# Attention by pairs of maps on row tiles of TensorE, values as weights, and the convolution's taps moved into the input projection

## The chip, the cores and the metric

The kernel runs on one core of a Trainium2 chip, in one launch. The time is the device time of that launch in microseconds; smaller is better. The core has TensorE (PE in the profile), VectorE (DVE), ScalarE (ACT), GpSimd (POOL) and SyncE (SP). Each engine runs its own list of instructions in order, and they meet at semaphores. Transfers run on 16 DMA engines, which the queues of SP, ACT and POOL feed.

## The reference

Two layers of a transformer step for 512 latent tokens and 128 context tokens of width 1024, all in f32. A layer is, in short:

```python
h = _rms(x, p['norm1_g']) * (1.0 + sc1) + sh1
u = h @ p['w_in']
qa, ka, va, pool_in, glu_in, qd, kd, vd = jnp.split(u, SPLIT_POINTS, axis=-1)
# A: 4 query heads on 2 key heads of 64, q/k norm, rotary:  p = softmax(s); o = p @ v
# D: 4 heads, two maps each (32 features):  p = softmax(s1) - lam * softmax(s2); o = p @ v, then _rms over 64
# B: means over windows of 2, 4, 8, 16 tokens, minus x, times pool_w
# C: a * sigmoid(gate), 31-tap depthwise convolution, norm over 256 channels, silu, pw_w
m = jnp.concatenate([o_a, o_b, o_c, o_d], axis=-1) @ p['w_out']
x = x + g1 * m
h2 = _rms(x, p['norm2_g']) * (1.0 + sc2) + sh2
x = x + g2 * _expert_choice_ffn(h2, ...)   # 16 experts, top-k tokens each, SwiGLU
```

Shift, scale and gate (sh, sc, g) are six products of silu(c) with w_mod. Latent queries see 128 cached keys and 512 latent keys, context queries the 128 context keys. So there are 12 score maps (4 of A, 8 of D) for each of 4 latent row tiles of 128 x 640, and 12 of 128 x 128 for the context tile.

## The kernel before

Tokens stand in five row tiles of 128 (`t` = 0 to 3 latent, 4 context). A layer runs in five phases, with a barrier over all four computing engines at the end of each (`finish_phase`).

Phase 1, the input projection. The order of its steps is written by hand (`ORDER` for TensorE, `TAKE_ORDER` for the engines that empty PSUM). "x": a tile of x, already scaled by VectorE, is turned by 8 transposes (L399) and taken into `H` (features x tokens), half by ScalarE (L805), half by VectorE (L1082). "s": squares of a later x tile (L797). "j": 24 matmuls of a row tile with w_in give q, k, v (L422 to L424), then squares, root on GpSimd (L1389), gains and rotary. "q": seven transposes bring q and k into `qkT`. "f": the pooling and convolution columns come out with features on the partitions (L453, L454), last of all. x has two buffers.

Phase 2, attention. For each map TensorE multiplies a query tile, spread by GpSimd so that rows of other heads are zero (L1448, L1452), with all 128 rows of keys (L486 latent keys, L487 cached keys). VectorE takes the maximum (L1178), ScalarE the exponential with its sum (L877), TensorE turns the map in five chunks (L500), ScalarE copies them out (L885), and TensorE multiplies with the values, the turned map as weights and 64 value columns moving (L517). Once a row tile VectorE divides by the sums, subtracts the second maps and, with GpSimd's root, norms the differential heads; four transposes (L525) put the outputs into `H`. Between maps VectorE does the convolution's taps (L1214, 47 of 62), GpSimd the pooling sums and the other 15 taps (L1496, L1497).

Phase 3: mean and variance of the convolution by matmuls with `mean_w` (L560), norm, the modulations GATE1 and SCALE2 (L361), Silu, point-wise and pooling matmuls, and, among them, 16 instructions of the first tile's output projection (L547).

Phases 4 and 5: output projection, second norm, router, top-k; then a loop over 16 experts (L659, L667), whose weights stream through the six slots of `ring`.

## Time and profile before

| | us |
|---|---|
| median of 3 runs (lowest, highest) | 2118.03 (2117.74, 2120.58) |
| the profiled execution | 2116.8 |
| its span | 2114.7 |
| TensorE busy, of the span | 1922.1 |
| VectorE / ScalarE / GpSimd busy | 558.8 / 514.5 / 456.3 |
| mean granted TensorE clock | 0.948 |

The page gives TensorE as busy for 91% of the span, but that is a mean over stages of different kinds: the expert loops (530 to 1060 us and from 1558 us on) hold half of the span, with DMA at 99% or more in most slices. The stages of the change are from 36 to 400 us and from 1068 to 1435 us. A busy TensorE in them says that it sets the pace only where its instructions follow each other without a gap and the others wait for it, so the timeline and the idle times of the other engines are read beside the busy share.

### The profile page before, as it was taken

Reading aid. Unit: us, or ns where it says so; the run is one execution under the profiler, and the core shown is the slowest. Engines: PE = TensorE matmul, PEld = TensorE weight load, DVE = VectorE, ACT = ScalarE, POOL = GpSimd, SP = SyncE. Lnnn points to the kernel's source line nnn. Section 1 sums busy time; section 2 is a strip of 40 time slices with the busy share of each in tenths; the row PEclk is TensorE's granted clock in tenths of the full one; section 3 lists DMA queues with packets and bytes.
Section 4 is the critical chain, followed back from the end, with each engine's and each line's share of the span. In section 5 each row is a group of like instructions: output and inputs, shape, how many; then the busy total and the mean of one; then the engine's idle time right before and its main releaser. Section 6 shows DMA issues by size and latency. Waiting matters only on the chain.

```text
span 2114.7 us, 40059 instructions
## 1 busy us (share of the span) xinstructions
PE 1922.1 (91%) x17136; PEld 1008.8 (48%) x17136; DVE 558.8 (26%) x1087; ACT 514.5 (24%) x1266; POOL 456.3 (22%) x411
## 2 busy tenths in 40 slices
PE   4999997995999999999969999979759999999994
PEld 1555886452344444444435568844424444444442
DVE  1331776234011110111113147742320101101111
ACT  1111553211221221221211135531112212212122
POOL 0221755000111111111112155520001111111112
PEclk9999997996999999999979999969879999999997
DMA  9401200727799999999961040035339999999996
GB/s 384 175 1 75 93 1 1 299 90 286 282 401 398 395 404 396 396 403 396 404 254 57 0 167 1 1 151 198 140 125 383 404 396 396 403 396 404 396 395 237
DMA packets 146264, 538.38 MB, mean 255 GB/s; under 512 B 8272, under 2 KB 14512, under 8 KB 145936
## 3 DMA queue, kind: packets, MB, share of 16 engines
q1 hardware_dynamic: 118512, 468.88, 55.7%
q10 hardware_dynamic: 14112, 42.56, 5.4%
q0 software_dynamic: 13568, 25.96, 5.1%
q8 instruction: 48, 0.79, 0.2%
q14 instruction: 24, 0.20, 0.0%
HBM read 510.86 MB, written 26.64 MB: 254 GB/s over the span
## 4 chain that ended last, share of the span: by engine, by line
PE 73%; DMA 17%; DVE 4%; issue 1%; ACT 1%; SPq 1%; POOL 1%; POOLq 0%; ACTq 0%; DVEq 0%
PE PS L659 23%; DMA ring<-in_exp_w_up 12%; PE PS L667 11%; PE PS L547 7%; PE PS L517 5%; PE PS L486 4%; PE PS L453 4%; PE PS L422 3%; PE PS L423 3%; PE PS L500 3%; PE PS L424 2%; PE PS L361 1%; DMA ring<-in_w_mod 1%; SPq L307 1%; DMA x_rows<-arena 1%
## 5 line engine op out<-in xcount | busy, mean ns | idle before, releaser
L659 PE MATMUL PS<-ring,arena 128*32 128x512 f32 x6144 | 684.0, 596 | 15.5 <-ACT gate_rows L769 9.2
L659 PEld LDWEIGHTS PS<-ring,arena 128*32 128x32 f32 x6144 | 201.9, 110 | 436.7 <-issue 410.2
L667 PE MATMUL PS<-ring,arena 128*32 128x256 f32 x6144 | 349.5, 379 | 0.0
L667 PEld LDWEIGHTS PS<-ring,arena 128*32 128x32 f32 x6144 | 205.4, 110 | 167.1 <-issue 56.7
L1529 POOL DMA_INDIRECT x_rows<-arena x64 | 102.5, 1601 | 648.1 <-DVE arena L1349 598.0
L985 ACT ACTIVATE arena<-PS,modB,modA 128x64 f32<-128x64 f32 x272 | 84.0, 413 | 391.9 <-PE PS L646 391.9
L547 PE MATMUL PS<-ring,H 128*128 128x512 f32 x320 | 142.5, 604 | 1.7 <-ACTq L737 1.7
L1515 POOL DMA_INDIRECT arena<-xn_rows,arena x68 | 68.1, 1001 | 344.4 <-DVE arena L1335 255.7
L1388 POOL TENSOR_SCALAR stat<-stat 128x1 f32<-128x1 f32 (+2 forms) x45 | 13.4, 299 | 524.9 <-ACT arena L950 223.3
L486 PE MATMUL PS<-arena,H 128*128 128x512 f32 x192 | 103.0, 618 | 7.9 <-POOL H L1448 5.8
L517 PE MATMUL PS<-arena 128*128 128x64 f32 x816 | 108.1, 273 | 1.8 <-DVE arena L1192 1.6
L1009 ACT ACTIVATE arena<-PS 128x512 f32<-128x512 f32 x32 | 19.1, 597 | 364.3 <-PE PS L659 364.3
L517 PEld LDWEIGHTS PS<-arena 128*128 128x128 f32 x816 | 104.8, 198 | 2.6 <-DVE arena L1192 2.1
L1178 DVE TENSOR_REDUCE stat<-PS 128x1 f32<-128x640 f32 (+1 forms) x120 | 85.9, 716 | 61.0 <-PE PS L487 55.8
L1214 DVE SCALAR_TENSOR_TENSOR arena<-arena,par 128x655 f32<-128x655 f32 x90 | 100.5, 1117 | 0.0
L453 PE MATMUL PS<-H,ring 128*128 128x512 f32 x192 | 98.3, 594 | 0.0
L885 ACT ACTIVATE arena<-PS 128x640 f32<-128x640 f32 (+1 forms) x120 | 74.1, 617 | 98.9 <-PE PS L500 98.3
L547 PEld LDWEIGHTS PS<-ring,H 128*128 128x128 f32 x320 | 61.5, 195 | 75.9 <-issue 73.8
L877 ACT ACTIVATE arena<-PS,stat 128x640 f32<-128x640 f32 (+1 forms) x120 | 84.6, 705 | 52.3 <-DVE stat L1181 52.0
L1339 DVE TENSOR_TENSOR arena<-arena,PS 128x512 f32<-128x512 f32 x32 | 22.0, 688 | 271.0 <-PE PS L659 271.0
L422 PE MATMUL PS<-ring,H 128*128 128x512 f32 x160 | 83.9, 606 | 7.7 <-DMA ring<-in_w_in 7.7
L1334 DVE COPY arena<-arena 128x2 f32 x32 | 5.4, 169 | 292.9 <-POOLq L1532 257.9
(193 smaller groups left out, 1983.8 us busy)
## 6 DMA issues: line engine op xcount, KB each, us to landing
ring<-in_exp_w_gate SPq DMA_DIRECT2D x64, 2048.0 KB, 17.6
ring<-in_exp_w_up SPq DMA_DIRECT2D x64, 2048.0 KB
ring<-in_exp_w_down SPq DMA_DIRECT2D x64, 2048.0 KB
ring<-in_w_mod SPq DMA_DIRECT2D x18, 2048.0 KB, 8.2
ring<-in_w_in SPq DMA_DIRECT2D x8, 2048.0 KB, 25.4
arena<-in_w_mod ACTq DMA_DIRECT2D x6, 2048.0 KB, 14.2
ring<-in_w_out SPq DMA_DIRECT2D x4, 2048.0 KB
arena<-x_rows ACTq DMA_DIRECT2D x15, 512.0 KB, 6.4
```

The costliest lines, as they stand in the source:

```text
L422: mm(PS[:, b0, :], lhs, ring[:, s, kk, 0:512], start=(k == 0), stop=(k == KD - 1))
L453: mm(PS[:, 2 + 2 * ((n + 2) % 3), :], lhs, H[:, k, 0:LAT], start=(k == 0), stop=(k == KD - 1))
L486: mm(PS[:, b0, :], lhs, qkT[:, kc, 0:LAT], start=True, stop=True)
L517: last = mm(PS[:, 6 + o0 // 512, o0 % 512:o0 % 512 + HD], PT[:, n % 2, c * P:(c + 1) * P], v, start=(c == 0), stop=(c == chunks - 1))
L547: last = mm(PS[:, 2 * (t % 2) + c, :], H[:, k, t * P:(t + 1) * P], ring[:, 4 + k // 4, k % 4, c * 512:(c + 1) * 512], start=(k == 0), stop ...
L659: last = mm(PS[64 * c + r:64 * c + r + LANE, bank, :], left[:, c0 + r:c0 + r + LANE], ring[:, s0 + k // 4, k % 4, c * HALF:(c + 1) * HALF] ...
L667: last = mm(PS[32 * j:32 * j + 32, bank, 0:QUART], left[:, c0:c0 + 32], ring[:, s0 + k // 4, k % 4, j * QUART:(j + 1) * QUART], start=(k = ...
L877: do(Pm[:, n % 3, 0:w], pair(2 * (n % 2), w), ACT.Exp, bias=stat[:, 8 + n % 4:9 + n % 4], scale=(HD ** -0.5 if gqa else 32 ** -0.5), accum ...
L985: do(xeT[:, c0:c0 + 64], PS[:, 7, c0:c0 + 64], ACT.Identity, bias=modB[:, 1, 0, k:k + 1], scale=modA[:, 1, 0, k:k + 1])
L1178: link(V.reduce_max(stat[:, 44 + n % 2:45 + n % 2], pair(2 * (n % 2), w), AX.X))
L1214: link(V.scalar_tensor_tensor(y3[:, i, :], u[:, i, k:k + OUTW], cwT[:, i, k:k + 1], y3[:, i, :], ALU.mult, ALU.add))
L1529: pool.indirect_dma_start(x_parts[m], bass.IndirectOffsetOnAxis(ap=idxc[:, p, m:m + 1], axis=0), yb[:, SPAN[m]], None, compute_op=ALU.add) ...
```

## The change

- Projection: x has a buffer for each of its five tiles, all five are loaded at once, turned and taken first; in layer 0 ScalarE takes the modulation rows ahead of the squares. Then come the first j step and the first f step in halves, the other f steps in a new order (`F_ORDER`), then the j and q steps. VectorE does 36 convolution taps between them and 19 more in the j steps, GpSimd 7 taps and the pooling. w_in's loads alternate between its halves. The states are written behind the last q step.
- Attention: work goes by 30 pairs of maps (`PAIRS`), in a list that also holds the convolution's norm and point-wise matmuls, the pooling mixes and the head norm (`ITEMS`). The two maps of a pair are multiplied on different rows of the array, straight from `qkT`; cached keys come spread from memory (`kcS`). GpSimd multiplies by one over the sum, VectorE subtracts the second map from the first in SBUF. Four units a row tile (two heads each) are turned in pieces A, B and C and multiplied with the values as weights, so that the output has features on the partitions already. The head norm's sums and its scales go through TensorE.
- Phase 3 is gone; its modulations are the third item of the attention. The output projection is in one piece behind the barrier. w_out's first 256 rows are put in another order on the host.

The diff, cut to its core:

```diff
-    PHASES = 5
+    PHASES = 4
...
+        xt = [poolD[:, 0:D], y[:, 0:D]] + [soft[:, i * D:(i + 1) * D] for i in range(3)]
...
-        OUT_AT = 15
-        DVE_TAPS = 16
+        DVE_TAPS = 24
...
+        PAIRS = (("gqa", 0), ("diff", 0), ("diff", 1), ("gqa", 1), ("diff", 2), ("diff", 3))
+        UNITS = (("gqa", 0, 0), ("diff", 0, 2), ("gqa", 1, 3), ("diff", 1, 5))
+        def attention_items():
+            items = []
+            for n in range(6 * LT):
+                items.append(("p", n))
+                if n == 1:
+                    items.append(("mean", 0))
+                if n == 3:
+                    items.append(("var", 0))
+                if n in (10, 16, 22):
+                    items.append(("sa", (n - 10) // 6))
+                if n in (13, 19):
+                    items.append(("sb", (n - 13) // 6))
+            items += [("p", 24), ("p", 25), ("sb", 2), ("p", 26), ("p", 27), ("pw", 0), ("p", 28), ("pw", 1),
+                      ("p", 29), ("mix", 0), ("sa", 3), ("mix", 1), ("sb", 3), ("sa", 4), ("sb", 4)]
+            return items
...  TensorE, projection
+                for t in range(NT):
+                    step_x(l, t)
+                for ks in (range(0, 4), range(4, KD)):
+                    step_j(l, 0, ks)
+                    step_f(l, 0, ks)
+                for i in range(1, 6):
+                    step_f(l, i)
+                for t in range(1, NT):
+                    step_j(l, t)
+                    step_q(l, t - 1)
+                step_q(l, LT)
...  TensorE, attention
+                def set_free(l, k):
+                    if k < 2:
+                        return
+                    kind, x = ITEMS[k - 2]
+                    if kind == "p":
+                        pe.wait_ge(t_exp, 2 * NP * l + 2 * x + 2)
...
+                def scores(l, k, n):
+                    t, r = divmod(n, 6)
+                    kind, i = PAIRS[r]
+                    area = set_at(k)
+                    for m in range(2):
+                        if kind == "gqa":
+                            rows, qc, kc = slice(64 * m, 64 * m + 64), i, 2
+                        else:
+                            r0 = 32 * (2 * (i % 2) + m)
+                            rows, qc, kc = slice(r0, r0 + 32), 3 + i // 2, 5 + i // 2
+                        lhs = qkT[rows, qc, t * P:(t + 1) * P]
+                        if t == LT:
+                            last = mm(area[:, 896 * m:896 * m + P], lhs, qkT[rows, kc, LAT:TOK], start=True, stop=True)
+                        elif m == 0:
+                            mm(area[:, P:512], lhs, qkT[rows, kc, 0:LAT - P], start=True, stop=True)
+                            left, right = lhs, qkT[rows, kc, LAT - P:LAT]
+                        else:
+                            mm(area[:, 1024:1536], lhs, qkT[rows, kc, 0:LAT], start=True, stop=True)
+                    if t < LT:
+                        mm(area[:, 512:640], left, right, start=True, stop=True)
+                        for m in range(2):
+                            last = mm(area[:, 896 * m:896 * m + P], qkT[:, i if kind == "gqa" else 3 + i // 2,
+                                                                        t * P:(t + 1) * P],
+                                      kcS[:, 0 if kind == "gqa" else 1 + i, m * P:(m + 1) * P], start=True, stop=True)
+                    last.then_inc(t_scores, 1)
...
+                def multiply_values(l, v, chunk, pt):
...
+                        last = mm(PS[64 * i:64 * i + 64, 7, 0:P], val, pt[:, i * P:(i + 1) * P],
+                                  start=(chunk == 0), stop=(chunk == 4 or t == LT))
+                def piece_b(l, v):
+                    pe.wait_ge(u_e01, 4 * LT * l + v + 1)
+                    turn_maps(l, v, (4,), PS[:, 6, :]).then_inc(u_T4, 1)
+                    pe.wait_ge(u_e23, 4 * LT * l + v + 1)
+                    for chunk in range(4):
+                        multiply_values(l, v, chunk, (PT01, PT23)[chunk // 2][:, 256 * (chunk % 2):][:, 0:256])
...
+                    elif kind == "mean":
+                        pe.wait_ge(c_y, l + 1)
+                        channel_mean(k, y3, c_mean)
+                        modulate(l, GATE1, 6)
+                        modulate(l, SCALE2, 7)
...  ScalarE, projection
-                squares(l, 0)
-                squares(l, 1)
                 for b, bank in FIRST_MODS[l]:
                     take_mod(l, b, bank)
+                squares(l, 0)
+                for t in range(NT):
+                    if t + 1 < NT:
+                        squares(l, t + 1)
+                    step_x(l, t)
...  VectorE, projection
+                step_j(l, 0)
+                step_f(l, 1)
+                conv_taps(16)
+                step_f(l, 3)
+                conv_taps(20)
+                for t in range(1, NT):
+                    step_j(l, t)
+                    step_q(l, t - 1)
+                    if t == 2:
+                        add_mod(l, SHIFT2, 7)
+                    conv_taps(5 if t < LT else 4)
+                step_q(l, LT)
...  VectorE, attention, for each item
+                    if kind == "p":
+                        maximum(l, k, x)
+                        if x >= 1:
+                            reciprocals(l, x - 1)
...
+                    for v, which in PIECES[k]:
+                        piece(l, v, which)
+                    if kind == "p" and 2 <= x < 29:
+                        subtract_maps(l, x - 2)
```

How the instruction lists change is shown at three places. A name ahead of the arrow is what is written, `PS` is PSUM, `arena` holds most of SBUF's working tiles, and a row in brackets names the semaphores it waits for. The first is TensorE in the middle of the attention, before, one latent map and the next:

```order
L486 MATMUL PS<-arena,H 128x512 [waits t_exp]
L487 MATMUL PS<-par,H 128x128
L500 MATMUL PS<-ident,arena 128x128 [waits t_pt,t_exp]
L500 MATMUL PS<-ident,arena 128x128 x4
L517 MATMUL PS<-arena 128x64 [waits t_pt]
L517 MATMUL PS<-arena 128x64 x3
L517 MATMUL PS<-par,arena 128x64
```

and after, one pair of maps with its pieces B and C:

```order
L586 MATMUL PS<-arena 128x384 [waits t_exp]
L589 MATMUL PS<-arena 128x512
L591 MATMUL PS<-arena 128x128
L593 MATMUL PS<-arena 128x128 x2
L639 MATMUL PS<-ident,H 128x128 [waits u_e01]
L639 MATMUL PS<-ident,H 128x128
L666 MATMUL PS<-arena 64x128 [waits u_e23]
L666 MATMUL PS<-arena 64x128 x7
L666 MATMUL PS<-arena,par 64x128 [waits u_e4]
L666 MATMUL PS<-arena,par 64x128
```

A map's own scores, transposes and values gave way to two maps' scores and a share of a unit's transposes and values, with more waits in between. The second place is ScalarE at the start of layer 0, before:

```order
L797 ACTIVATE arena,stat<-arena 128x1024 [waits x_loaded0]
L797 ACTIVATE arena,stat<-arena 128x1024 [waits n_ss,x_loaded1]
L755 ACTIVATE modrow<-PS 128x256 [waits slot_used5]
L755 ACTIVATE modrow<-PS 128x256 [waits slot_used3]
L805 ACTIVATE H<-PS,modB,modA 128x128 [waits scales_set,n_xT]
L805 ACTIVATE H<-PS,modB,modA 128x128 x3
```

and after:

```order
L888 ACTIVATE modrow<-PS 128x256 [waits slot_used5]
L888 ACTIVATE modrow<-PS 128x256 [waits slot_used3]
L930 ACTIVATE arena,stat<-arena 128x1024 [waits x_loaded0]
L930 ACTIVATE arena,stat<-arena 128x1024 [waits n_ss,x_loaded1]
L938 ACTIVATE H<-PS,modB,modA 128x128 [waits scales_set,n_xT]
L938 ACTIVATE H<-PS,modB,modA 128x128 x3
```

The squares (L797, now L930) moved behind both modulation rows. The third place is TensorE around the barrier between projection and attention, after:

```order
L503 MATMUL PS<-ident,arena 128x128 [waits b0_evac,b1_evac,rd_done,ra_done]
L503 MATMUL PS<-ident,arena 128x128 x6
L503 MATMUL PS<-ident,arena 128x128 [waits b0_evac,b1_evac,p_ds,ra_done]
L503 MATMUL PS<-ident,arena 128x128 x6
L586 MATMUL PS<-arena 128x384 [waits f_mm,kc_loaded,params_loaded,phase_done]
```

and before:

```order
L453 MATMUL PS<-H,ring 128x512
L454 MATMUL PS<-H,ring 128x128
L453 MATMUL PS<-H,ring 128x512
L454 MATMUL PS<-H,ring 128x128
L486 MATMUL PS<-arena,H 128x512 [waits f_mm,q_spread,params_loaded,phase_done]
```

The last work of the projection was an f step, with nothing of a q step behind it; now it is the last q step.

## Rows read from the trace of the kernel before

**Rows 1.** The page's chain that ended last, shares of the span.

```profile
PE 73%; DMA 17%; DVE 4%; issue 1%; ACT 1%; SPq 1%; POOL 1%; POOLq 0%; ACTq 0%; DVEq 0%
```

**Rows 2.** Windows of layer 0: length, engines busy (x count), PEclk, DMA share, GB/s.

```profile
201.00:226.00 25.00, 21.03 (x133) 16.33 (x133) 17.57 (x29) 12.20 (x25) 21.66 (x21) 1.00 0.86 336
204.00:365.00 161.00, 147.27 (x993) 122.11 (x994) 121.08 (x213) 83.15 (x190) 103.91 (x77) 0.94 0.13 51
365.00:400.50 35.50, 31.82 (x189) 15.64 (x188) 8.93 (x12) 10.43 (x14) 0.00 (x0) 0.84 0.61 237
```

**Rows 3.** Timeline of PE in one latent map: start us, us, engine, line.

```profile
211.81 1.08 PE L486 MATMUL PS<-arena,H 128*128 128x512 f32 x2
...
212.94 0.71 PE L500 MATMUL PS<-ident,arena 128*128 128x128 f32 x5
...
213.49 1.00 PE L517 MATMUL PS<-arena 128*128 128x64 f32 x8
...
214.55 1.08 PE L486 MATMUL PS<-arena,H 128*128 128x512 f32 x2
```

**Rows 4.** Chain of waits, output projection, then one expert: start us, us.

```profile
400.54 20.87 PE PS L547 x48
...
587.34 7.00 PE PS L659 x64
594.35 3.45 PE PS L667 x64
...
619.90 7.06 PE PS L659 x64
```

**Rows 5.** Groups by line and shape, layer 0: count, busy us, mean ns.

```profile
L1214 DVE SCALAR_TENSOR_TENSOR arena<-arena,par 128x655 f32<-128x655 f32 x45 | 50.3, 1117 | 0.0
L1178 DVE TENSOR_REDUCE stat<-PS 128x1 f32<-128x640 f32 x48 | 39.5, 823 | 28.0 <-PE PS L487 27.9
...
L1345 DVE COPY arena<-PS 128x512 f32<-128x512 f32 x16 | 11.1, 691 | 1.6
...
L877 ACT ACTIVATE arena<-PS,stat 128x640 f32<-128x640 f32 x48 | 37.9, 790 | 18.8 <-DVE stat L1181 18.7
...
L1496 POOL TENSOR_SCALAR arena<-arena,par 128x655 f32<-128x655 f32 x14 | 31.2, 2232 | 2.3 <-POOL arena L1497 2.1 <-POOL arena L1493 0.2
...
L1497 POOL TENSOR_TENSOR arena<-arena 128x655 f32<-128x655 f32 x14 | 25.1, 1793 | 2.6 <-POOL arena L1496 2.6
...
L877 ACT ACTIVATION_READ_ACCUMULATOR arena<-PS,stat 128x1 f32 x59 | 11.8, 201 | 0.0
```

**Rows 6.** Windows in the context tile's attention.

```profile
340.00:342.00 2.00, 0.99 (x7) 0.85 (x7) 1.86 (x7) 0.02 (x1) 0.19 (x1) 1.00 0.00 0
342.00:344.00 2.00, 1.33 (x5) 1.14 (x5) 0.90 (x3) 0.60 (x3) 1.86 (x2) 0.59 0.00 0
...
352.00:354.00 2.00, 1.12 (x7) 0.98 (x7) 1.44 (x5) 0.81 (x5) 1.85 (x1) 0.85 0.00 0
```

**Rows 7.** Timeline of layer 0: projection's start, its end, first score matmul.

```profile
49.44 2.05 PE L422 MATMUL PS<-ring,H 128*128 128x512 f32 x2 [7.73 <-DMA ring<-in_w_in]
...
201.14 4.67 SPq L307 DMA_DIRECT2D ring<-in_w_mod  x4
...
203.91 1.10 PE L486 MATMUL PS<-arena,H 128*128 128x512 f32 x2 [2.90 <-POOL H L1448]
```

**Rows 8.** Timeline ahead of the projection, layer 0, then layer 1.

```profile
36.42 0.38 ACT L755 ACTIVATE modrow<-PS 128x256 f32<-128x256 f32 x1 [13.06 <-PE PS L361]
...
46.98 1.49 ACT L805 ACTIVATE H<-PS,modB,modA 128x128 f32<-128x128 f32 x4
...
1075.02 1.06 ACT L797 ACTIVATE arena<-arena 128x1024 bf16<-128x1024 f32 x1 [22.12 <-DMA arena<-x_rows]
...
1077.69 1.06 ACT L797 ACTIVATE arena<-arena 128x1024 bf16<-128x1024 f32 x1 [1.52 <-DMA arena<-x_rows]
...
1083.89 1.92 PE L422 MATMUL PS<-ring,H 128*128 128x512 f32 x2
```

More of the change, by code:

```diff
@@ new lines, in attention_pieces @@
+        def attention_pieces(items):
+            waiting = [(v, piece) for v in range(NU) for piece in (("A", "B", "C") if v < 4 * LT else ("A", "C"))]
+            out, n = [], -1
+            for i, (kind, x) in enumerate(items):
+                n = x if kind == "p" else n
+                now = []
+                room = 2 if n < 24 else 4
+                if kind == "sa":
+                    assert not waiting or waiting[0][0] > 4 * x + 3, x
+                if (kind, x) == ("mix", 1):
+                    now, waiting = waiting, []
+                while waiting and len(now) < room and unit(waiting[0][0])[3] + 3 <= n:
+                    now.append(waiting.pop(0))
+                out.append(now)
+            assert not waiting
+            return out
```

894 lines of the change are left out of this document (474 added, 420 removed).

## The prediction

> **What bounds the kernel now.** I read the page first, from the chain that ended last: 73% of it is TensorE, 17% a DMA [rows 1]. The chain in order of time then shows two kinds of stage. In the expert loop an expert takes 619.90 - 587.34 = 32.6 us of matmuls [rows 4], and later the weights set the pace; the change doesn't touch this, nor what is in the ring when it starts, and I cost it at nothing. What is left is, for each of two layers, the stretch from the first transposed row of x to the start of the output projection. The windows show layer 0's attention: TensorE busy 147 of 161 us, VectorE 121, ScalarE 83, GpSimd 104, and 35.5 us behind it for the convolution's norm, the mixes and a first part of the output projection [rows 2]. The timeline of one latent score map shows why TensorE is the bound there: maps follow each other in 214.55 - 211.81 = 2.74 us, without a gap: 1.13 us of scores, 0.55 us of transposes, 1.06 us of values [rows 3]. 48 such maps are 131.5 us. Layer 0 has its projection from 49.4 to 201.1, its first score matmul at 203.9 [rows 7], and the output projection running alone from 400.5 [rows 4]: 196.6 us from the first score matmul to there. Layer 1 is a copy of it.
>
> **TensorE's part of the attention.** A matmul in f32 is two instructions; one with 512 columns takes 20.87/48 = 0.43 us [rows 4], so a column costs 0.84 ns per instruction. A pair of maps has 1280 score columns, 2 x 1280 x 0.84 = 2.15 us if they run in turn, as now. In the new kernel the two maps of a pair lie on different rows of the array. No row shows row tiles. The nearest are column tiles: 64 instructions of 512 columns on four 32-column tiles take 7.0 us, 0.11 us each against 0.43 alone [rows 4], so four run at once. If two row tiles do so too, the 1024 spread columns cost 0.86 and the 256 columns of cached context, which keep all rows, 0.43: 1.29 us. I take that; 2.15 is the other end. Transposes fall from 60 to 40 a tile, as the differential maps are subtracted before they are turned: 40 x 0.11 = 4.4 us. Values become weights of 64 columns on two column tiles: 80 instructions of 128 columns a tile, 0.107 each in turn or half that at once, 8.6 or 4.3 us. Together 6 x 1.29 + 4.4 + 4.3 = 16.4 us a tile, against 32.9 now. So TensorE stops being the bound and the waits between engines set the pace.
>
> **The new period.** The other engines for a pair: the maximum over 1280 elements from PSUM, 0.82 us for 640 [rows 5], so 1.49; two exponentials of 0.79 + 0.20, 1.9; GpSimd's scaling, 2.2 for 655 elements by two scalars, about 2.6 for 1280; VectorE's subtraction 1.12 beside a busy GpSimd; copies of 512 columns 0.69 [rows 5]. No engine is full (VectorE some 9.5 of 12.6 us). The order on VectorE makes a closed path over three pairs, with pieces (A, B), (C, A), (B, C): maximum 1.49, reciprocal 0.2, copy of chunks 2 and 3 0.7, to TensorE 0.15, values 0.86, scores of the next pair 1.29, back 0.27, maximum 1.49, reciprocal and output copy 0.5, to TensorE 0.15, two chunks turned 0.43, back 0.27, copy 0.7, subtraction 1.12, maximum 1.49, reciprocal and output copy 0.5, subtraction 1.12: 12.7 us, or 4.2 a pair. (The small ones are estimates from the same kind of rows.) TensorE works 8.1 of the 12.7 us, in bursts with gaps of nearly 2 us. [...] At the low clock its 8.1 us are 16.2 and with the waits a pair takes 6.0. I take one pair in six at it: 4.5 us a pair. The ends are 4.2 and, with the low clock for most of the time, 5.4.
>
> [...]
>
> **The sum from first score matmul to output projection.** The first two pairs, the mean, and the two modulations now between them: 18.5 us (cold TensorE, 64 instructions each modulation 3.6; their weights, 8.4 MB at 336 GB/s [rows 2], need about 22 us from the release of the ring, and lie within the tail told below). Pairs 2 to 5 with the second mean, logarithm and exponential, gate and its round trip: 21. Eighteen pairs at 4.5: 81. Five small items of the head norm between them: 4.5. Then the end: pairs 24 to 29, two Silus with table loads, point-wise matmuls, mixes, last pieces, and the last norm, a chain of 5.5 us over four engines: 38. That is 163. The part of the output projection that was inside the old stage (16 instructions, 6.9) follows now: 169.9 against 196.6, **26.7 us less a layer**. The convolution's norm (35.5 us window) is what leaves, not hidden for nothing: its VectorE and ScalarE work stands in the 21 and 38.
>
> **What the change adds ahead.** First, all five x tiles are turned and taken out before any projection, where three were turned among the matmuls. ScalarE does, in order, squares of tile t+1 (1.06 + 0.2) and tile t's half of the eviction (1.49) [rows 8]: 2.75 us a tile. In layer 0 its first squares now stand behind the last modulation row, 36.4 [rows 8]; squares, root, scaling, transposes and five steps of 2.75 end 19.4 us after 36.8, at 56.2, and 1.5 MB of x loaded earlier push the modulation's weights by 3.9 us: start at 60.1 instead of 49.4 (+10.7). In layer 1 x arrives at 1075.0 and 1077.7; the same chain ends at 1094.4 instead of 1083.9 [rows 8] (+10.5). Second, the projection itself: 151.7 us now [rows 7]; minus 24 transposes of x and 14 of the last two q steps, and 2 us of waits, it ends its last j step at 145.5. But behind that now stands a tail that the f steps covered: square, reduce, root (3.7), gains and copy (3), four convolution taps on VectorE at 1.12 (4.5) [rows 5], the copy of the last q, lambda's exponential with a table load (2.1), four state DMAs issued by ScalarE (1.6), barrier: 15.6, so the first score matmul comes 161.1 us after the start instead of 154.5 (+6.6). GpSimd's two last taps, 2 x (2.2 + 1.8) [rows 5], end beside it. The 55 taps of VectorE otherwise lie beside dense matmuls and cost nothing: 17.9 us a row tile against some 14 of VectorE. If that cover fails (36 taps within 5 f steps of 8.6), up to 5 us. Per layer +17.2; both ends: +10 if the loads overlap better, +22.
>
> **Total.** 2 x (17.2 - 26.7) = -19 on the profiled execution's 2116.8 us (span 2114.7 and 2.1 around it), which is 1.2 under the median: 2118.0 - 19 = **2099 us**.
>
> **Rivals.** (a) The clock holds: a pair takes 4.2 and the end 34, 9.4 less a layer: 2080. For it: 1.00 throughout the latent tiles, at gaps there of nearly none; against it rows 6. (b) Slower: the halves of a pair run in turn. Scores 2.15, values 1.72; TensorE is the bound again with its waits, 5.6 a pair, 18 x 1.1 + 3 = 23 more a layer: 2145. It is slower than before from 5.0 a pair. For it: no row shows row tiles; against it the column tiles. Here the change would not do what it says. (c) The clock is low for most of the attention: 5.4 a pair and 3 more at the end, 19 a layer: 2137. (d) Two instructions of one tile stand behind each other and hold up the next tile: only the second pass of a map and the first of the next overlap, 0.32 + 0.43 + 0.43 + 0.43 = 1.6 us of scores; half of that on the path and more of TensorE's time, 0.3 a pair: 2110. The column tiles of rows 4, with the same pairs of instructions, speak against it.
> [...]
>
> **Chances.** Forecast 0.45, (a) 0.22, (b) 0.13, (c) 0.14, (d) 0.06. Within 0.2% (4 us) is about what can't be told from no change. Of the forecast's own range, 2082 to 2120, nearly a quarter lies above 2110; so faster is nearly all of (a), most of (d) and of the forecast: 0.64; same 0.12; slower, (b) and (c) less a little: 0.24. The range for 8 in 10: 2072 to 2138.
>
> **What would show it.** Right: score matmuls of the two halves overlap; latent pairs every 4.2 to 4.8 us; projections that start 10 us later in each layer and a gap of 12 to 16 us between them and the scores; VectorE and TensorE each idle a third of the attention. Wrong: a period above 5; PEclk near 0.5 there; a gap below 8 us; an expert loop that is not the same length.

## The result: 0.8% slower, where 0.9% faster was forecast

The changed kernel takes 2134.28 us (median of 4 runs, 2133.36 to 2138.27) against 2117.89 us (4 runs, 2115.28 to 2120.58): the ratio is 1.0081, 95% interval 1.0063 to 1.0099. Its profiled execution spans 2131.6 us, 16.9 more than the one of before. The forecast was 2099, and 64 of 100 for faster; the range, 2072 to 2138, holds the time.

The page of the changed kernel, shares of the chain that ended last:

```profile
PE 66%; DMA 18%; DVE 5%; ACT 3%; issue 3%; SPq 1%; POOL 1%; POOLq 1%; ACTq 0%; DVEq 0%
```

TensorE's share fell from 73% [rows 1] to 66%: it is busy for 1845.3 us of the execution, where it was 1922.1, and more of the chain now runs through other engines. The events that answer to those of [rows 4, 7, 8], from the timeline of the changed kernel (start us, us, engine, line, operation, count, and in brackets the idle time before with its releaser); first layer 0:

```profile
59.42 2.07 PE L486 MATMUL PS<-ring,H 128*128 128x512 f32 x2 [1.59 <-ACT H L938]
...
217.59 0.59 PE L488 MATMUL PS<-ring,H 128*128 128x256 f32 x2
...
232.76 1.00 PE L586 MATMUL PS<-arena 64*128 64x384 f32 x1 [7.28 <-ACTq L872]
...
396.91 3.78 PE L723 MATMUL PS<-ring,H 128*128 128x512 f32 x4 [0.62 <-DVEq L1173]
...
536.07 1.94 PE L794 MATMUL PS<-ring,arena 128*32 128x512 f32 x8 [4.62 <-ACT gate_rows L902]
...
1075.17 2.28 ACTq L881 DMA_DIRECT2D arena<-x_rows  x5
1102.04 2.07 PE L486 MATMUL PS<-ring,H 128*128 128x512 f32 x2 [1.59 <-ACT H L938]
...
1259.90 0.59 PE L488 MATMUL PS<-ring,H 128*128 128x256 f32 x2
...
1278.10 1.00 PE L586 MATMUL PS<-arena 64*128 64x384 f32 x1 [10.32 <-POOLq L1535]
```

In layer 1 the output projection then starts at 1441.35 and the experts at 1574.44. In the kernel before, the x loads of layer 1 were issued at 1068.26, its first score matmul came at 1238.20, the output projection ran alone from 1435.01, and the experts began at 530.82 and 1558.79. So, in us, layer 0 / layer 1:

| stretch | before | after | difference | forecast |
|---|---|---|---|---|
| up to the first j matmul (layer 1: from the x loads) | 49.4 / 15.6 | 59.4 / 26.9 | +10.0 / +11.2 | +10.7 / +10.5 |
| first j matmul to first score matmul | 154.5 / 154.3 | 173.3 / 176.1 | **+18.9 / +21.8** | +6.6 |
| first score matmul to output projection alone | 196.6 / 196.8 | 164.2 / 163.3 | -32.5 / -33.6 | -33.6 |
| from there to the first expert | 130.3 / 123.8 | 139.2 / 133.1 | +8.9 / +9.3 | +6.9 |
| experts | 537.4 / 555.9 | 539.1 / 557.2 | +1.7 / +1.3 | 0 |

The attention came out within 1.2 us of the forecast. One row is wrong, and by more than all the others together: from the first j matmul to the first score matmul, which is the projection and the tail behind it. A list of what TensorE waited for between the first j matmul and the first score matmul of layer 0 (us in total, times, longest) names it:

```profile
PE PS L486 <- DVE mod L1183: 9.5, 1, 9.5
PE PS L586 <- ACTq L872: 7.3, 1, 7.3
PE PS L503 <- DVE arena L1257: 4.8, 1, 4.8
```

The second and the third are the tail that the prediction had priced. The first, 9.5 us, is in no step of it. Layer 1 has the same row with the same 9.5. The timeline at that place, TensorE and then VectorE:

```profile
169.26 0.93 PE L503 MATMUL PS<-ident,arena 128*128 128x128 f32 x7
170.03 0.38 PE L433 MATMUL PS<-ident,modrow 128*128 128x128 f32 x2
179.90 2.05 PE L486 MATMUL PS<-ring,H 128*128 128x512 f32 x2 [9.49 <-DVE mod L1183]
```

```profile
170.22 0.55 DVE L1222 TENSOR_REDUCE stat<-arena 128x6 f32<-128x384 f32 x1 [0.33 <-ACT arena L948]
173.08 0.42 DVE L1227 TENSOR_TENSOR arena<-PS,stat 128x256 f32<-128x256 f32 x1 [2.31 <-POOL stat L1566]
...
178.16 1.05 DVE L1253 TENSOR_TENSOR arena<-arena 128x384 f32<-128x384 f32 x1
179.12 0.55 DVE L1257 COPY arena<-PS 128x384 f32<-128x384 f32 x1
179.59 0.16 DVE L1183 TENSOR_TENSOR mod<-PS,pTs 128x16 f32<-128x16 f32 x1
```

Read them together. TensorE turns the second tile's q and then the row SHIFT2 (L433), into the PSUM bank that the fourth row tile's j step will use. That step waits until VectorE has added the turned row (L1183, 0.16 us of work). But VectorE has the third tile's j step first in its program: reduce, a root fetched from GpSimd, gains, rotary, 8.9 us; then the copy of q; then the addition. TensorE stands idle, and its next two matmul instructions take 2.05 us instead of 1.02. The windows ahead of the gap, of the gap and behind it (PEclk is the third number from the end) show the granted clock fall from 0.98 to 0.50:

```profile
59.00:170.00 111.00, 110.58 (x414) 60.55 (x415) 63.41 (x65) 8.87 (x23) 43.86 (x34) 0.98 0.15 59
170.00:180.00 10.00, 0.51 (x5) 0.30 (x3) 7.37 (x12) 1.44 (x5) 8.23 (x8) 0.78 0.00 0
180.00:182.00 2.00, 2.00 (x3) 0.97 (x4) 1.93 (x3) 0.00 (x0) 1.99 (x1) 0.50 0.03 8
```

The same wait is in the kernel before, but its VectorE had the other order, q and the addition first:

```profile
110.66 0.56 DVE L1127 COPY arena<-PS 128x384 f32<-128x384 f32 x1 [6.91 <-PE PS L437]
111.13 0.16 DVE L1053 TENSOR_TENSOR mod<-PS,pTs 128x16 f32<-128x16 f32 x1
...
114.55 0.55 DVE L1092 TENSOR_REDUCE stat<-arena 128x6 f32<-128x384 f32 x1 [0.72 <-ACT arena L815]
```

The attention, on the other hand, does what was said. Four latent pairs of layer 0 and the start of a fifth on TensorE (L586 and L589 are the spread scores of the two maps, L593 the cached context):

```profile
289.64 0.59 PE L586 MATMUL PS<-arena 64*128 64x384 f32 x1
289.65 0.69 PE L589 MATMUL PS<-arena 64*128 64x512 f32 x1
290.07 0.48 PE L586 MATMUL PS<-arena 64*128 64x384 f32 x1
290.18 0.59 PE L589 MATMUL PS<-arena 64*128 64x512 f32 x1
290.39 0.38 PE L591 MATMUL PS<-arena 64*128 64x128 f32 x2
290.70 0.71 PE L593 MATMUL PS<-arena 128*128 128x128 f32 x4
...
293.84 0.58 PE L586 MATMUL PS<-arena 32*128 32x384 f32 x1
...
297.00 0.61 PE L624 MATMUL PS<-rows_of,arena 128*128 128x2 f32 x4
298.89 0.58 PE L586 MATMUL PS<-arena 32*128 32x384 f32 x1 [1.28 <-ACT H L1016]
...
302.90 1.09 PE L666 MATMUL PS<-arena 128*64 128x128 f32 x16 [0.68 <-DVE arena L1349]
303.93 0.59 PE L586 MATMUL PS<-arena 64*128 64x384 f32 x1
...
308.13 0.58 PE L586 MATMUL PS<-arena 32*128 32x384 f32 x1
```

Within a pair the two maps' matmuls start 0.01 us apart and run side by side; the first map's second instruction (290.07) starts after the second map's first one (289.65). Pairs follow in 4.20, 5.05, 5.04 and 4.20 us. In the 5.05 stands a small item of the head norm (L624), which takes one of the two score areas, so that the next scores wait 1.28 us for the exponentials. The 5.04 has no such item: there TensorE has 26 instructions of transposes and values, against 12 in the 4.20, and waits 0.68 us for VectorE's copy of two turned chunks (L1349). From the pair at 289.64 on three pairs take 14.3 us (once 14.9), with one item among them, or 4.8 a pair; the three ahead of it, which have none, take 4.85, 3.16 and 5.04, 13.1 together, where the prediction's closed path had 12.7. The windows of a stretch of latent pairs, and of the tail behind the last j step (length, busy PE, PEld, DVE, ACT, POOL, PEclk, DMA share, GB/s):

```profile
275.00:350.00 75.00, 61.12 (x496) 44.69 (x492) 42.39 (x67) 34.12 (x80) 26.92 (x19) 0.96 0.00 1
218.00:233.00 15.00, 2.92 (x17) 2.28 (x17) 9.59 (x16) 4.06 (x9) 9.61 (x7) 0.68 0.67 246
```

### The profile page after: what moved, and what is told of

Its sections match the earlier page's. It is cut to its first block, busy times and chain, and to the rows that moved or that the text cites. A ratio compares the mean times of both kernels' runs of the same rounds, so it can differ in the third digit from the quotient of the medians.

```text
span 2131.6 us, 38834 instructions
## 1 busy us (share of the span) xinstructions
PE 1845.3 (87%) x16748; PEld 920.7 (43%) x16748; DVE 591.4 (28%) x1035; ACT 470.8 (22%) x1208; POOL 449.6 (21%) x410
## 4 chain that ended last, share of the span: by engine, by line
PE 66%; DMA 18%; DVE 5%; ACT 3%; issue 3%; SPq 1%; POOL 1%; POOLq 1%; ACTq 0%; DVEq 0%
PE PS L794 22%; DMA ring<-in_exp_w_up 15%; PE PS L802 11%; PE PS L723 7%; PE PS L527 4%; PE PS L486 4%; PE PS L487 3%; PE PS L586 2%; PE PS L488 2%; PE PS L425 2%; PE PS L666 2%; DMA ring<-in_w_mod 1%; PE PS L593 1%; SPq L369 1%; PE PS L639 1%
## 5 line engine op out<-in xcount | busy, mean ns | idle before, releaser
L723 PE MATMUL PS<-ring,H 128*128 128x512 f32 x320 | 142.7, 606 | 1.2 <-DVEq L1173 1.2
L1275 DVE SCALAR_TENSOR_TENSOR arena<-arena,par 128x655 f32<-128x655 f32 x106 | 121.9, 1150 | 3.5
L486 PE MATMUL PS<-ring,H 128*128 128x512 f32 x160 | 87.3, 629 | 22.1 <-DVE mod L1183 19.0
L1324 DVE TENSOR_REDUCE stat<-PS 128x2 f32<-128x1280 f32 (+1 forms) x60 | 76.6, 1277 | 107.4 <-PE PS L593 98.0
L487 PE MATMUL PS<-ring,H 128*128 128x512 f32 x160 | 85.1, 614 | 0.0
L1501 DVE SCALAR_TENSOR_TENSOR arena<-PS,arena 128x512 f32<-128x512 f32 x32 | 24.0, 751 | 213.2 <-PE PS L794 213.2
L1120 ACT ACTIVATE arena<-PS,modB,modA 128x32 f32<-128x32 f32 x272 | 78.1, 438 | 0.0
L586 PE MATMUL PS<-arena 32*128 32x384 f32 (+1 forms) x96 | 47.2, 574 | 31.1 <-POOLq L1535 10.3
L1016 ACT ACTIVATE arena<-PS,stat 128x640 f32<-128x640 f32 (+1 forms) x88 | 58.7, 674 | 35.7 <-DVE stat L1324 35.7
L425 PE MATMUL PS<-ring,scT 128*32 128x256 f32 x576 | 36.7, 413 | 28.8 <-ACT scT L919 19.1
```

The lines of the kernel that those rows point to most:

```text
L425: last = mm(PS[32 * q:32 * q + 32, bank, 256:512], scT[:, k, :], slot(s)[:, kk, q * 256:(q + 1) * 256], start=(k == 0), stop=(k == KD - 1))
L486: mm(PS[:, b0, :], lhs, ring[:, s, kk, 0:512], start=(k == 0), stop=(k == KD - 1))
L487: mm(PS[:, b0 + 1, :], lhs, ring[:, 2 + s, kk, 256:768], start=(k == 0), stop=(k == KD - 1))
L586: mm(area[:, P:512], lhs, qkT[rows, kc, 0:LAT - P], start=True, stop=True)
L723: last = mm(PS[:, 2 * (t % 2) + c, :], H[:, k, t * P:(t + 1) * P], ring[:, 4 + k // 4, k % 4, c * 512:(c + 1) * 512], start=(k == 0), stop ...
L1120: last = do(xeT[:, HALF + c0:HALF + c0 + 32], PS[:, 1, QUART + c0:QUART + c0 + 32], ACT.Identity, bias=modB[:, 1, 1, k:k + 1], scale=modA[ ...
```

## The experiments

The theory: the 9.5 us, and the slow restart behind them, in each layer turn a gain into a loss, and they come from the order of two steps on VectorE alone. The first rival: VectorE, with 55 more taps in the projection, is simply full, and the wait shows up wherever it is next needed. The second, carried over from the prediction: the halves of a pair don't gain what they should. All comparisons are with the kernel before on the same chip, whose median was 2116.46 to 2118.21 us in these runs.

**Turned late.** The wait goes, since nobody needs the bank any more:

```diff
-                        if t == 3:
-                            pe.wait_ge(mod_added, mod_n(l, SHIFT2))
 # step_q of TensorE
-                    if t == 1:
+                    if t == 3:
                         pe.wait_ge(p_v, NT * l + t + 1)
                         turn_mod(l, SHIFT2, 7)
 # VectorE
-                    if t == 2:
+                    if t == 4:
                         add_mod(l, SHIFT2, 7)
```

> Edit to the changed kernel: the turned row of the second shift (SHIFT2) is made after the last j step instead of between the third and the fourth, VectorE adds it there, and the fourth j step no longer waits for that addition. Theory (a wait of TensorE on VectorE in the projection): in the changed kernel TensorE stands still for 9.5 us in each layer between the third and the fourth j step, and comes back at the low clock (its first matmuls 2.05 us for 1.02). Both go: the last j step ends about 147.5 us after the first begins, for 158.6, 11 us less a layer, and the whole is 2134 - 2 x 11.5 = 2111 (2107 to 2115). Rival (VectorE is full with its 55 taps, so the wait only moves to the next step that needs VectorE): the last j step ends within 3 us of 158.6, the whole 2128 to 2134.

Measured: 2110.63 us (10 runs, 2104.12 to 2112.93), ratio to before 0.9971 (0.9961 to 0.9981). The stretch of j and f steps is 12.6 and 11.8 us shorter in the two layers; TensorE's only waits there are the start and the tail, as listed for layer 0:

```profile
PE PS L584 <- ACTq L870: 7.4, 1, 7.4
PE PS L501 <- DVE arena L1255: 4.6, 1, 4.6
PE PS L484 <- ACT H L936: 1.6, 1, 1.6
```

The theory holds, and VectorE isn't full: no other wait took the place. With so small an edit the change is 0.3% faster than before instead of 0.8% slower.

**VectorE's order.** Nothing moves on TensorE; VectorE takes the turned q and row first:

```diff
                 for t in range(1, NT):
+                    if t == 2:
+                        step_q(l, t - 1)
+                        add_mod(l, SHIFT2, 7)
                     step_j(l, t)
-                    step_q(l, t - 1)
-                    if t == 2:
-                        add_mod(l, SHIFT2, 7)
+                    if t != 2:
+                        step_q(l, t - 1)
```

> Edit to the changed kernel, on VectorE alone: for the third row tile it takes the second tile's turned q and adds the turned SHIFT2 before, not after, its own nine microseconds of work for that j step, as the kernel before has it. Nothing moves on TensorE. Theory (the stall is made by VectorE's order): the wait of TensorE before the fourth j step falls from 9.5 us to about 1.5 (the copy 0.55, the addition 0.16 and two signals), its clock isn't lost: 8 to 10 us less a layer, the whole 2134 - 18 = 2116 (2112 to 2120), 3 to 5 above the kernel that turns late. Rival (VectorE is full, the wait moves): 2128 to 2134, with new waits on VectorE in the fourth and the fifth j step.

Measured: 2111.53 us (12 runs, 2108.97 to 2116.71), ratio 0.9976 (0.9967 to 0.9985). The wait is still there and costs 0.7 us a layer:

```profile
PE PS L486 <- DVE mod L1183: 0.7, 1, 0.7
```

It was 0.8 us shorter than expected, and the time lies 0.5 us under the range that was expected; the two remedies can't be told apart by their times. The cause is the order, not the work.

**The same fault put into the kernel before.** One line of its hand-written order:

```diff
-              ("q", 1), ("x", 4), ("j", 2), ("q", 2), ...
+              ("j", 2), ("q", 1), ("x", 4), ("q", 2), ...
```

> Edit to the kernel before: in the order in which VectorE, ScalarE and GpSimd take the projection's results, the third tile's j step comes ahead of the second tile's q step and the fourth's x step (before: q 1, x 4, j 2; now: j 2, q 1, x 4). TensorE's order and all the work stay. Theory (it is the order that makes the stall, taps or no taps): TensorE waits for the addition of SHIFT2, and for the eviction of q 1, about 9 us in each layer ahead of the last x tile and the fourth j step, and restarts at the low clock, 9 to 11 us a layer: 2118 + 20 = 2138 (2134 to 2142), with no other part of the change present. Rival (VectorE is idle 7 us there in the kernel before, so its order is free; the stall needs the taps): 2118 within 3.

Measured: 2139.27 us (4 runs, 2132.01 to 2140.87), ratio 1.0110 (1.0095 to 1.0126). TensorE of this kernel in layer 0:

```profile
111.48 0.38 PE L369 MATMUL PS<-ident,modrow 128*128 128x128 f32 x2
120.46 1.94 PE L399 MATMUL PS<-ident,arena 128*128 128x128 f32 x8 [8.61 <-DVE arena L1127]
122.20 1.92 PE L422 MATMUL PS<-ring,H 128*128 128x512 f32 x2
```

8.6 us idle in each layer, and transposes and matmuls at the low clock behind it (granted 0.50 from 120.46 to 124.5 us in layer 0). From the first j matmul to the last matmul of the projection it is 11.0 and 9.0 us more. The medians are 21.7 us apart, without a row tile, a pair, or a tap in the projection; the profiled execution is the fastest of the four. The step of the order is worth more than the whole change.

**Without the taps.** On the kernel that turns late; 53 of VectorE's 55 taps are left out, so the convolution isn't computed in full:

```diff
                     for _ in range(n):
-                        conv_tap(*taps.pop(0))
+                        i, k = taps.pop(0)
+                        if k == 0:
+                            conv_tap(i, k)
```

> The kernel that turns late (the edit of the first run of this series), and VectorE's convolution taps left out but for the first of each half: 53 of 55 are missing, so the convolution isn't computed in full; all else stays. It tests the forecast's claim that these 60 us of VectorE beside the projection cost nothing. Theory (covered by TensorE): the projection's dense part as long as with the taps, within 1 us a layer; of the tail behind it VectorE's four taps go (5.3 us), but ScalarE's four output DMAs and GpSimd's last tap come next, so 0 to 4 us a layer: the whole 1 to 8 us under the kernel that turns late. Rival (VectorE's load holds TensorE up all over, and GpSimd with it): more than 12 us under it.

Measured: 2108.90 us (6 runs, 2104.77 to 2111.28), ratio 0.9964 (0.9952 to 0.9976), 1.7 us under the kernel that turns late. The windows of the projection, that kernel first, then the one without taps:

```profile
59.00:205.00 146.00, 145.48 (x515) 79.34 (x516) 88.00 (x96) 12.39 (x33) 67.78 (x57) 0.98 0.12 45
```

```profile
59.00:205.00 146.00, 145.85 (x514) 79.54 (x515) 31.95 (x45) 12.02 (x32) 61.77 (x57) 0.98 0.12 45
```

56 us less on VectorE, and TensorE is busy for 145.5 or 145.9 of 146 us either way. From the first j matmul to the end of the last it is 146.2 and 146.7 us with the taps, 147.1 and 146.1 without them. That the taps beside the matmuls cost nothing was right; four of them stand in the tail.

**Both maps on the same rows.** On the kernel that turns late, the second map takes the first one's rows of the array, so that the result is another:

```diff
-                            rows, qc, kc = slice(64 * m, 64 * m + 64), i, 2
+                            rows, qc, kc = slice(0, 64), i, 2
-                            r0 = 32 * (2 * (i % 2) + m)
+                            r0 = 32 * (2 * (i % 2))
```

> The kernel that turns late, and both maps of a pair take queries and keys from the rows of the first map: 0 to 63 of the array for the grouped heads, the same 32 for the differential ones. The second map's scores are then those of the first, so the result isn't attention; the instructions, their columns and all waits are the same. It prices the row tiles. Theory (row tiles run side by side): the 1024 spread columns cost 1.72 instead of 0.86 us a pair, 24 pairs, most of it on the chain: 15 to 20 us a layer, the whole 2110.6 + 35 = 2146 (2130 to 2152). Rival (the halves don't really run together, what the trace shows is only the order of issue, or a pair waits for other engines anyway): 2110.6 within 6.

Measured: 2169.23 us (4 runs, 2164.49 to 2172.43), ratio 1.0253 (1.0236 to 1.0269), 59 us above the kernel that turns late: outside the range that was expected, on the theory's side. A pair's scores in this kernel:

```profile
302.69 0.91 PE L584 MATMUL PS<-arena 64*128 64x384 f32 x2
303.44 1.02 PE L587 MATMUL PS<-arena 64*128 64x512 f32 x2
304.30 0.38 PE L589 MATMUL PS<-arena 64*128 64x128 f32 x2
304.61 0.71 PE L591 MATMUL PS<-arena 128*128 128x128 f32 x4
```

From the first matmul to the context part it is 304.61 - 302.69 = 1.92 us here and 290.70 - 289.64 = 1.06 with row tiles: 0.86 us a pair, the forecast's number, 20.6 us for 24 pairs. But from the first score matmul to the output projection a layer takes 27.6 us more (163.5 to 191.1, and 164.4 to 192.0). The windows from one to the other, that kernel first, then the one on the same rows:

```profile
220.00:384.00 164.00, 128.38 (x972) 88.49 (x972) 80.84 (x144) 72.91 (x171) 49.88 (x40) 0.90 0.22 88
```

```profile
220.00:411.00 191.00, 162.90 (x971) 108.14 (x971) 83.62 (x144) 72.90 (x171) 48.56 (x40) 0.83 0.19 75
```

The same number of instructions, 34.5 us more of TensorE, at a granted clock of 0.83 for 0.90. In windows of 0.5 us, the same stretches show 1.00 or 0.50 in 362 of 382 windows here (0.50 in 120) and in 316 of 328 in the kernel that turns late (0.50 in 62). So the shares that are missing from 1.00 are some 65 us at 0.50 for some 33 (an estimate from the two means: 191 x 0.17 x 2 and 164 x 0.10 x 2). That the 7 us beyond 20.6 are this clock is likely, but no run shows it by itself, nor why the clock is lower while TensorE is busier.

**The start.** On the kernel that turns late, the x tiles go back among the matmuls (with the waits that this needs):

```diff
-                for t in range(NT):
-                    step_x(l, t)
-                for ks in (range(0, 4), range(4, KD)):
-                    step_j(l, 0, ks)
-                    step_f(l, 0, ks)
-                for i in range(1, 6):
+                step_x(l, 0)
+                step_j(l, 0, range(0, 4))
+                step_x(l, 1)
+                step_x(l, 2)
+                step_j(l, 0, range(4, KD))
+                step_x(l, 3)
+                step_x(l, 4)
+                for i in range(6):
```

> The kernel that turns late, and in it the x tiles go back among the matmuls: x 0, first half of j 0, x 1, x 2, second half of j 0, x 3, x 4, then the six f steps in a row (in the changed kernel: five x tiles, then j 0 and f 0 in alternate halves). It prices the later start. Theory (the start stands on ScalarE's 2.75 us a tile, which a j step of 17.2 us can cover): layer 1's first j matmul comes 13 us earlier after the load of x than in the kernel that turns late, layer 0's 6 to 8 us (held by w_in then); 32 transposes, 3.5 us, move behind it; so 9.5 and 4 us: 2110.6 - 13.5 = 2097 (2093 to 2101). Rival (ScalarE and VectorE can't bring the later tiles in time, TensorE waits at x 2 to x 4 and at f 0, or the clock falls in the gaps): less than 5 us in all, 2106 to 2111.

Measured: 2100.16 us (5 runs, 2094.29 to 2100.61), ratio 0.9917 (0.9904 to 0.9931), 10.5 us under the kernel that turns late. The j steps start 12.7 and 12.9 us earlier, as expected in layer 1 and sooner than expected in layer 0, but the stretch of j and f steps grows by 8.5 and 5.6 us where 3.5 for transposes was counted. In both layers the first f step waits 2.1 us for the last x tile, which with the transposes is all of layer 1's 5.6:

```profile
72.83 1.66 PE L528 MATMUL PS<-H,ring 128*128 128x512 f32 x2 [2.12 <-ACT H L941]
```

In layer 0 TensorE is also at the low clock (granted 0.52 from 46.8 to 53.0 us) for 6.0 us behind the first j matmul instead of 4.1, and again behind this wait (0.57 from 73 to 77). The profiled execution is the fastest of the five; its attention is 3.2 and 2.8 us shorter than in the kernel that turns late, with nothing changed there. Its mean granted clock was 0.942, that of the three executions near 2100 was 0.937; so the medians' 10.5 us are the better measure than the profiles' 16, and the stretches that were changed give 12.7 + 12.9 - 8.5 - 5.6 = 11.5.

**The tail.** On the kernel that turns late, in short:

```diff
 # VectorE
-                conv_taps(20)
+                conv_taps(24)
...
+                    if t == LT: ...   # lambda's sums, ahead of the last j step
-                    conv_taps(5 if t < LT else 4)
+                    conv_taps(5 if t < LT else 0)
 # ScalarE: lambda's exponential ahead of the last j step, the state DMAs ahead of step_q(l, LT)
 # GpSimd: no tap behind its last j step
```

> The kernel that turns late, and the tail between projection and scores shortened: VectorE's last four taps are taken 24 instead of 20 after the fourth f step, lambda's sums and exponential before the last j step, ScalarE issues the four state DMAs before its last copy of q, GpSimd's last three taps stand before its last j step (in the changed kernel one before and two behind). No work is left out. Theory (the tail is the sum of these, behind the nine microseconds of the last q step): what is left is q's own chain, about 7.5 us, and the barrier: the gap from last j matmul to first score falls from 16 and 19 us to 9 to 10 in each layer, 2110.6 - 15 = 2096 (2092 to 2100). Rival (the weights of the modulations and a slow release of GpSimd at the barrier hold it, 5.5 us from its last tap to its signal in layer 1, not the taps): the gap of layer 1 stays above 15 us, 2103 to 2107.

Measured: 2102.38 us (6 runs, 2101.11 to 2107.21), ratio 0.9934 (0.9921 to 0.9948), 8.2 us under the kernel that turns late, between the range of the theory and that of the rival; one of GpSimd's taps overwrites pooling sums, so the pooled channels of its second half aren't the reference's. The gap from the end of the last j matmul to the first score fell from 14.7 to 8.2 and from 17.7 to 9.3 us (the expectation counts it from 1.3 us earlier): the 15 us that were expected. But over a third is given back: the stretch from the first score matmul to the output projection grew from 163.5 to 167.7 and from 164.4 to 166.0. TensorE now waits in the attention's third item, in layer 0:

```profile
PE PS L426 <- DMA ring<-in_w_mod: 4.0, 2, 3.2
```

In layer 1 it is 2.9 us. The 8.4 MB for two modulations start when the projection releases the ring, so a shorter tail moves part of the wait behind it.

**All three.** The three edits in one kernel; the first overwrites the sums as above, the second has GpSimd's taps in another place, and computes everything.

> The three edits together: turned late, x tiles among the matmuls, tail shortened. All work is done. Theory (three separate stretches of the chain, nothing shared): the gains add, 2134 - 23.5 - 13.5 - 15 = 2082 (2076 to 2090), 1.7% under the kernel before. Rival (VectorE or GpSimd, with 40 taps between the fourth f step and the second j step, become late when TensorE no longer waits): 2090 to 2097.

> The three edits together again, with two of GpSimd's three last taps ahead of its second j step and one behind its fourth. In the run before this one they shared a buffer with the pooling sums, so that its result was another; all else is as there. Theory: where GpSimd's taps stand, ahead of the last j step, does not matter: 2096 (2092 to 2099), gap from last j matmul to first score 9.5 and 10.6 us, attention 169 us a layer, 5 more than with the long tail, because TensorE now waits 3.6 us for the weights of the two modulations and starts the pairs behind them at the low clock. Rival (two taps ahead of the second j step make GpSimd late there): TensorE waits at the second q step, 2099 to 2104.

Measured: 2096.04 us (5 runs, 2092.59 to 2097.22), ratio 0.9897 (0.9883 to 0.9911), and 2093.77 (6 runs, 2091.23 to 2099.23), ratio 0.9893 (0.9875 to 0.9910). So the place of GpSimd's taps makes no difference that could be seen. The sum that was expected, 2082 (at most 2090), is missed, and the time lies in the range of the rival, late VectorE or GpSimd. That rival isn't borne out: TensorE's only waits in these projections are the start, the first f step's 2.1 us and the tail. The start gave 3 us and the tail 7 us less than expected, and together they give 2 to 4 us less than apart (2110.6 - 10.5 - 8.2 = 2091.9), which is about as much as the intervals leave open.

**The gate row earlier.** On the last one, half of the weights that the attention waited for are used in the projection:

```diff
+                load_mod(l, GATE1)         # SyncE, behind SHIFT2, ahead of w_out, same ring slots
...
+                        if t == 3:
+                            modulate(l, GATE1, b0 + 2)
...
 # the attention's third item
-                        modulate(l, GATE1, 6)
                         modulate(l, SCALE2, 7)
```

> As the run before it, and the modulation row GATE1 made earlier: its weights go through the third pair of ring slots behind SHIFT2 and ahead of w_out, its 64 matmuls stand before the fourth j step, its turn and addition behind SHIFT2's; in the attention only SCALE2 is left, and one load of 4.2 MB before it instead of two. No work is added. Theory (what the short tail lost in the attention is the wait for 8.4 MB of weights): TensorE no longer waits at the modulation, the attention falls from 169 to 161 to 163 us (64 matmuls, 3.6 us, leave it, and 3.6 of waiting), the projection grows by 3.6: 3.5 to 5 us a layer, 2096 - 8 = 2088 (2084 to 2092). Rival (the lost time was the low clock after a shorter tail, not the weights): attention 165 or more, 2093 to 2097.

Measured: 2084.92 us (5 runs, 2081.07 to 2085.18), ratio 0.9843 (0.9826 to 0.9859), the fastest here: 1.6% under the kernel before, 49 us under the changed one, and all is computed. The attention went from 168.1 to 159.6 and from 170.4 to 162.6 us, the projection grew by 4.0 and 3.3; in the list of TensorE's waits the row of the weights, 4.3 and 3.1 us before, is gone. What the shorter tail had lost was for the most part the wait for weights.

## Why the prediction was wrong

By its own steps, in order.

*TensorE's part of the attention, and its period.* Right. The costs that it starts from stand in the traces: in the changed kernel L591 is one matmul of a pair in the list and two instructions in the trace (290.39, x2), and in its projection two instructions of 512 columns take 0.85 us (L486 at 164.97, L487 at 165.82) and two of 256 take 0.44 (L488 at 166.68, L486 at 167.12): 0.83 to 0.86 ns a column. That column tiles run four at once is in the page of before (L659 on column tiles, L547 on the whole array):

```profile
L659 PE MATMUL PS<-ring,arena 128*32 128x512 f32 x6144 | 684.0, 596 | 15.5 <-ACT gate_rows L769 9.2
L547 PE MATMUL PS<-ring,H 128*128 128x512 f32 x320 | 142.5, 604 | 1.7 <-ACTq L737 1.7
```

One instruction takes 596 or 604 ns, but they follow each other in 684.0/6144 = 0.11 us on the column tiles and in 142.5/320 = 0.45 on the whole array. Row tiles run side by side (0.86 us a pair less, by the run on the same rows), the last eighteen latent pairs with their five items take 85.1 and 85.2 us (forecast 81 and 4.5), the clock in the latent pairs is 0.96 (from 275 to 350 us). The 4.5 us a pair have one pair in six at the low clock, at 6.0 us, and no run shows either number; what the traces show is a granted clock of 0.52 from 342 to 352 us in the context tile of the kernel before, two L486 instructions in 2.05 us at 0.50 instead of 1.02, and 4.8 us a latent pair. A pair's maximum took the 1.49 us that were counted (L1324), GpSimd's scaling of a grouped pair 2.93 for 2.6 (L1653). The sum from first score matmul to output projection, 163, came out at 164.2 and 163.3, but partly since errors cancel: to the third pair 21.0 and 20.0 us (forecast 18.5), pairs 2 to 5 22.9 in both layers (21), the end from the context tile's pairs on 35.2 and 35.3 (38). Rivals (b) and (d) are refuted by the rows of the pair (the maps side by side, the second map not held up by the first one's second instruction), (c) by the clock and (a) by the sum, though the end came nearer to its 34. TensorE and VectorE were each to be idle for a third: in 164 us of attention TensorE was busy for 128 and VectorE for 81.

*The start.* Right: +10.0 and +11.2 for +10.7 and +10.5.

*The projection.* This is the step that failed: "minus 24 transposes of x and 14 of the last two q steps, and 2 us of waits, it ends its last j step at 145.5". It ended at 158.8 (217.59 + 0.59 - 59.42) and 158.5. The transposes were counted, and VectorE's work was summed against TensorE's for a row tile (14 of 17.9 us) and found to fit. It does fit. But a sum of busy time says nothing about *which* result is ready when, and the waits that exist were not walked one by one through the new order of each engine. With the wait gone the stretch is 12.6 and 11.8 us shorter, 146.2 and 146.7, so this one wait, 9.5 us and the restart at the low clock, is 24.4 us of the 36 between forecast and measurement. What the prediction put ahead of the scores, 17.2 us a layer with ends of 10 and 22, came out at 28.9 and 33.0. The wait itself is old; new is only what stands ahead of the awaited instruction, and the prediction prices 2 us of waits that go and names none that stays.

*The tail*, 15.6 us: 14.6 in layer 0, 17.6 in layer 1. Right as a sum in layer 0; in layer 1 the barrier is released by GpSimd, 5.5 us after its last tap and 3 us after ScalarE, which no step has. One sum beside it is off: the modulations' 8.4 MB at 336 GB/s are 25 us, not 22, and don't lie within a tail of 15.6. In the changed kernel this cost nothing, since TensorE came to them 28 us after the last j matmul, at 246.27; with the shorter tail it was the wait for weights.

*The taps cost nothing.* Right beside the matmuls (without them the stretch is 0.9 us longer in layer 0 and 0.6 shorter in layer 1, for 56 us less of VectorE's work).

*Behind the attention*: 6.9 us was the number of instructions at full clock. 8.9 and 9.3 came; the first four matmul instructions take 3.78 us, at a granted clock of 0.50, behind an end of the attention in which TensorE works in pieces (21.1 of its last 32 us, at a granted clock of 0.85). 4.4 us in all.

*The experts*, 0: they took 1.7 and 1.3 us more. No run was made on that.

What is left of the 36 us, some 4, lies in the rest of the projection (0.7 and 1.2), the attention (1.5) and the tail (1.0). No rival of the prediction had the mechanism. Two ended on the slower side. Halves in turn would have cost even more than was written (27.6 for 23 us a layer), but didn't happen; nor did a low clock for most of the attention, 2137, which lies near the measured 2134 by luck. That the range holds the time is luck as well: its upper end was there for these two.

## What to carry to other kernels

When a stage's order is rewritten, take each wait of the engine that bounds it and look up the instruction that it waits for: what stands ahead of that one on its own engine, in the new order? Here a result of 0.16 us had 8.9 us of someone else's work put ahead of it, and the wait that this made cost 24.4 us in the two layers, more than the 19 that the whole change was to bring; sums of busy time can't show it. The gaps on TensorE that this order makes cost more than their length: 3.1 and 2.3 us on top of 9.5 here, with a granted clock of 0.50 behind the gap, and 2.4 and 0.4 on top of 8.6 in the kernel before with the fault put in. The 2.90 us ahead of the first score matmul of the kernel before [rows 7] didn't: its clock was 1.00 behind them [rows 2]. And the work taken out of the tail paid only until the load of weights that starts at the same event: of 15 us 5.8 were given back.

## What the runs showed of the hardware that was not expected

Two maps in turn, instead of side by side, cost 27.6 us a layer where their matmuls account for 20.6; the granted clock was 0.83 for 0.90. And GpSimd: in layer 1 its last tap ends at 1270.83 + 1.74 = 1272.57, but the barrier is released by it only at 1278.06, as the chain of waits shows (start us, us; L1535 is the drain that signals the barrier):

```profile
1270.80 7.26 POOLq L1535
```

In the kernel with all three edits its last instruction of that phase ends at 1227.07 and the first score matmul comes at 1232.61, after a wait for the same line of GpSimd: 5.5 us in both, with another instruction last and no tap near it. In layer 0 the same drain ends 0.07 us after GpSimd's last instruction. The kernel before has it too: in layer 1 GpSimd's last instruction of the phase ends at 1186.38 and its drain at 1191.86, but there the first score matmul comes only at 1238.20, so it cost nothing. What GpSimd does in these 5.5 us is open. In layer 1 of these kernels the end of GpSimd's last instruction is no measure of when the barrier opens.
